# Waiting for x by tiles, and rounding turned outputs one pass earlier, in a two-block transformer kernel

## The reference

```
h = rmsnorm(x, g_mix_norm)
proj = h @ w_in                       # (256 x 1024) by (1024 x 6664)
...
o = g[0] * o_compressed + g[1] * o_selected + g[2] * o_window
x = x + o.reshape(256, 1024) @ a_w_out
```

## Time and profile before

| what | value |
|---|---|
| time, median of 3 runs | 1104.09 us (1103.22 to 1106.47) |
| profiled execution: time, span | 1103.02 us, 1101.2 us |
| TensorE busy | 1093.2 us, 99% |
| VectorE, ScalarE, POOL busy | 620.5, 584.7, 139.1 us |
| TensorE's granted clock | 1.00 |
| DMA | 185.40 MB, mean 168 GB/s |

### The profile page before, as it was taken

How to read it: one execution, slowest core, us unless ns; L and a number is a source line. 1 busy time by engine, 2 the same in 40 slices (tenths; PEclk the granted TensorE clock), 3 DMA queues, 4 the chain that set the end, 5 groups by cost and what they waited for, 6 DMA issues and landing times.

```text
span 1101.2 us, 14119 instructions
## 1 busy us (share of the span) xinstructions
PE 1093.2 (99%) x5851; PEld 928.0 (84%) x5851; DVE 620.5 (56%) x687; ACT 584.7 (53%) x916; POOL 139.1 (13%) x203
## 2 busy tenths in 40 slices
PE   8999999999999999999999999999999999999998
PEld 6877888888999988888889888888889888888887
DVE  5544544467555545456667665555457866555442
ACT  6788654434555434346567364444447846444431
POOL 1031311110231100122320010000004400000000
PEclk9999999999999999999999999999999999999999
DMA  8843534455644555545141254554544345555451
GB/s 317 322 153 115 191 115 154 143 175 179 242 176 169 191 194 189 196 127 186 61 153 48 95 200 175 181 183 171 191 153 138 112 153 199 186 189 191 172 181 68
DMA packets 29232, 185.40 MB, mean 168 GB/s; under 512 B 3552, under 2 KB 3936, under 8 KB 9184
## 3 DMA queue, kind: packets, MB, share of 16 engines
q1 hardware_dynamic: 27344, 178.31, 45.6%
q0 software_dynamic: 1680, 5.92, 1.5%
q10 hardware_dynamic: 144, 0.26, 0.1%
HBM read 183.43 MB, written 1.05 MB: 168 GB/s over the span
## 4 chain that ended last, share of the span: by engine, by line
PE 94%; ACT 2%; DVE 2%; DMA 1%; SPq 0%; issue 0%; DVEq 0%
PE ps L590 24%; PE ps L593 24%; PE ps L592 24%; PE ps L570 5%; PE ps L724 3%; PE ps L643 3%; PE ps L642 3%; PE ps L641 3%; PE ps L705 3%; ACT t L1233 1%; DMA t<-in_w 1%; PE ps L945 1%; ACT t L1236 1%; DVE t L1836 1%; DVE t L1988 0%; PE ps L786 0%
## 5 line engine op out<-in xcount | busy, mean ns | idle before, releaser
L1836 DVE TENSOR_TENSOR t<-t 128x2048 fp32r<-128x2048 f32 (+8 forms) x287 | 414.4, 1458 | 341.9 <-ACT t L1236 339.7
L1236 ACT ACTIVATE t<-t 128x2048 fp32r<-128x2048 f32 (+7 forms) x255 | 337.9, 1348 | 278.8 <-PE ps L593 236.5
L590 PE MATMUL ps<-t 128*128 128x512 f32 (+2 forms) x1178 | 465.3, 395 | 2.2 <-DVE t L1879 1.5
L593 PE MATMUL ps<-t 128*128 128x512 f32 (+2 forms) x1178 | 457.4, 388 | 0.0
L592 PE MATMUL ps<-t 128*128 128x512 f32 (+2 forms) x1178 | 457.1, 388 | 0.2 <-DVE t L1836 0.2
L590 PEld LDWEIGHTS ps<-t 128*128 128x128 f32 x1178 | 221.3, 188 | 45.8 <-DVE t L1879 1.9
L593 PEld LDWEIGHTS ps<-t 128*128 128x128 f32 x1178 | 221.1, 188 | 45.7
L592 PEld LDWEIGHTS ps<-t 128*128 128x128 f32 x1178 | 221.5, 188 | 43.1 <-DVE t L1836 0.9
L2518 POOL TENSOR_TENSOR t<-t 128x32 f32<-128x32 f32 (+8 forms) x108 | 92.2, 865 | 505.2 <-ACT t L1233 449.0
L1233 ACT ACTIVATE t<-ps,t 128x256 f32<-128x256 f32 (+4 forms) x216 | 95.8, 453 | 90.8 <-DVE t L1988 45.2
L1836 DVE TENSOR_TENSOR t<-ps,t 128x512 fp32r<-128x512 f32 (+6 forms) x124 | 76.0, 633 | 27.6 <-ACT t L1236 25.2
(11 more groups left out here) (109 smaller groups left out, 543.2 us busy)
## 6 DMA issues: line engine op xcount, KB each, us to landing
t<-in_w SPq DMA_DIRECT2D x155, 1024.0 KB, 4.9
t<-in_w SPq DMA_DIRECT2D x12, 512.0 KB, 4.7
t<-in_w SPq DMA_DIRECT2D x5, 768.0 KB, 4.1
t<-in_g POOLq DMA_DIRECT2D x4, 512.0 KB, 9.4
t<-in_w SPq DMA_DIRECT2D x2, 640.0 KB, 3.8
t<-in_w SPq DMA_DIRECT2D x4, 256.0 KB, 4.4
t<-in_x SPq DMA_DIRECT2D x1, 1024.0 KB, 5.4
t<-in_memt POOLq DMA_DIRECT2D x1, 1024.0 KB, 9.8
```

The source lines that it names most:

```text
L590: e.matmul(o, sh, wh, start=k0 + j == 0, stop=False)
L593: t = e.matmul(o, sl, wh, start=False, stop=last and j == n - 1)
L1236: return e.activation(o, src, ACT.Copy, scale=scale)
L1836: return e.tensor_tensor(o, a, b, op)
```

## The change

Four edits. TensorE waits in chunks 1 to 3 for the rest of the one tile of x that the next products read. Chunk 3 is cut tile by tile by ScalarE and VectorE. SyncE issues the load of `m.X` when the first half of chunk 2 has landed. ScalarE writes the rounded part of the sparse attention's turned outputs in passes 25 and 29, at the start of the pass, ahead of the copy and the exponents; VectorE's part stays in passes 26 and 30.

```diff
 tensor_program
     gemm_first(x)
     for c in range(1, 4):
-        gemm(c, x, ready)
+        gemm(c, x, lambda k, h: after("lo of", "x", k))
 scalar_program
     split_gained("x", m.xT, "gmix", 1, m.HT)
-    cut(3)
+    cut_by_piece(3)
...
-        elif i in (26, 30):
-            split(("no", 0, (i - 26) // 4), m.o_lo[0][:, :, half((i - 26) // 4)])
+        elif i in (25, 29):
+            split(("no", 0, (i - 25) // 4), m.o_lo[0][:, :, half((i - 25) // 4)])
 vector_program
-    for c in range(3, 6):
+    cut_by_piece(3)
+    for c in range(4, 6):
         cut(c)
 sync_program
         if c == 3:
-            w.wait_ge(*after("ld", 2, 3))
+            w.wait_ge(*after("ld", 2, 1))
             e.dma_start(m.X[:], x_d.rearrange("o (h p) d -> p (o h) d", p=128)).then_inc(*whole(("ld x",)))
```

## The result

The changed kernel takes 1100.95 us (median of 8 runs, 1099.87 to 1102.63) beside 1103.89 us for the kernel before (8 runs, 1103.22 to 1106.47). The ratio is 0.9975, 95% interval 0.9966 to 0.9984, which is 2.9 us less: 0.27%. Timed again beside later experiments it took 1100.48 against 1103.62, ratio 0.9973 (0.9964 to 0.9983). The profiled execution has a span of 1099.2 and a time of 1101.06 us (before 1101.2 and 1103.02).

The account below looks back on a forecast made before the run. The prediction took TensorE, 94% of the chain, to bound the kernel, so only its stops count. Terms of 1.72 + 0 + 0 + 0.4 + 0.4 = 2.5 us took 1104.09 to 1101.6 us, range 1100.0 to 1104.3.

Parts of the forecast that it names:

- Edit 1: TensorE's stop between chunks 1 and 2, waiting for x's turned tiles, vanishes: gain 1.72 us, bounds 0 and 1.8.
- the slow restart: First product after TensorE's stop before chunk 2 takes 0.33 us instead of 0.23; 0.10 us gained if the stop goes.
- Edit 2: Chunk 3 on ScalarE and VectorE: cutting by tiles buys 0.16 to 2 us of margin and no time.
- Edit 3: x's load: issued 2.4 us earlier, landed at about 21.2 instead of 22.3; buys margin before chunk 5, no time.
- The mixing danger: First stage: x's megabyte mixes with chunk 2's second half and tile 7; full mixing would stop TensorE 2.0 us.
- rivals B and C: x shares DMA engines, TensorE stops in chunk 2: B 1103.3 us, chance 0.12; C, full mixing, 1104.8, chance 0.06.
- Rival C: Full mixing stops TensorE 2.0 + 0.1 us in chunk 2, plus block 27's held scores: 1104.8 us, chance 0.06.
- Edit 4, first place: Sparse attention, product of chunk 88 and values behind it: earlier rounding gains 0.4 us, bounds 0 and 0.77.
- Edit 4, second place: Sparse attention, before chunk 89: wait and restart vanish through an earlier join; gain 0.4 us, bounds 0 and 0.46.
- Rival A: Sparse attention: held copy, exponents of pass 25 and slip of pass 29 eat the rounding gain; 1102.4 us, chance 0.2.
- Sum: All edits: 1.72 + 0 + 0 + 0.4 + 0.4 = 2.5 us, giving 1101.6 us from 1104.09; chance 0.62.

Follow-up runs that it names:

- e2: Kernel before with only ScalarE's rounding of the turned outputs moved to passes 25 and 29: 1103.19 us, ratio 0.9992.
- e1: Kernel before with only the products of chunks 1 to 3 waiting for x's tiles one by one: 1103.12 us, ratio 0.9992.
- e3: Changed kernel with x issued only when the second half of chunk 2 has landed: 1102.40 us, ratio 0.9987.
- e4: Changed kernel with no wait before x's load, issued right behind chunk 3: 1101.05 us, ratio 0.9971.
- a0: Changed kernel as it is, timed again: 1100.48 us, ratio 0.9973.
- a7: Changed kernel with ScalarE's rounding in passes 25 and 29 behind the copy, ahead of the exponents: 1099.80 us, ratio 0.9967.
- e10: a7 with chunk 1 issued right behind chunk 0: 1101.50 us, ratio 0.9979.
- e9: Changed kernel with chunk 1 issued right behind chunk 0, without waiting for chunk 0's second tile: 1101.13 us, one run.
- e8: Changed kernel with POOL's two loads of constants issued only when x has landed: 1101.94 us, one run.
- e6: Changed kernel with VectorE's rest of the turned outputs also moved to passes 25 and 29: 1103.59 us, one run.

## Why the prediction was right, point by point

The forecast was 1101.6 us, 2.5 us less; measured were 2.9 and 3.1 us less. The mechanism was right for edits 1 and 4 and wrong for edit 3; the sizes follow.

- **Edit 1.** Right, in place and in size: 1.72 forecast, 1.78 from chunk 1's first product to chunk 5's. Tile 7 was ready 0.59 us before its time, where 0.49 was worked out. What I had not seen is what the gain is counted from. Before, the end of the stage hangs on the landing of chunk 2's second half: chunk 2 starts 2.81 us after it (16.91 to 19.72; in e2 2.80, 17.76 to 20.56). Now it hangs on chunk 0 and chunk 1's first tile, and its lateness (0.5 to 1.4 us of wait in seven of ten such profiles) goes into the time in full. By 2.81 us behind the landing at 17.33, the old order would have started chunk 2 at 20.14 in the execution profiled after, against 18.64: an estimate of 1.5 us, and 1.6 with the slow restart, where the forecast had 1.62 and 1.72.
- **Edit 2.** Right as far as it was tested: e1, with chunk 3 whole, has no wait in chunk 3.
- **Edit 3.** This is the step that failed, twice. "I take x as landed at about 21.2" was wrong by its rule: the hole of 0.3 MB at 18 to 19 us was taken for time that x gains. It was filled, and half of x's sixteen parts had landed by 21.2 (the eighth at 21.13, the ninth at 21.23). But ScalarE waits for the last part, and that one landed 2.9 us behind the last part of chunk 3 as before: the lagging part had no hole to fill. And the term "buys margin, no time" was too small. The rest of chunk 5 is done 9.84 us after x has landed (22.30 to 32.14 before, 26.65 to 36.49 in e2). Before, its second product came at 34.58, a margin of 2.4 us, and in e2, which has neither edit 1 nor edit 3, x came 3.5 us later than usual and went through that margin: the stop of 1.0 us. With edit 1 the margin is smaller, 0.4 us in e3's profile (33.85 to 34.26) and 0.8 in the changed kernel's, so the same late x would stop TensorE longer; no profile shows this happen. The highest runs of kernels that issue x late are 3.0 (before, its 30 runs beside e1 to e4), 1.6 (e1), 2.4 (e2) and 2.8 us (e3) above the median, those of kernels that issue it early 1.7 (changed), 0.6 (e4), 1.4 (a0), 0.4 (a7) and 0.6 (e10). Without edit 3 the median is 1102.40 (e3), with it 1100.95, 1101.05 (e4) and 1100.48. That earlier issue protects from a late x is argued from this and from one profile. Why four parts of x landed 3.5 us later there was not found, and the intervals of e3 (0.9977 to 0.9997) and a0 (0.9964 to 0.9983) overlap. A rival was not tested: the three highest runs of e3 (1103.86 to 1105.20) and the eight highest beside e1 to e4 of the kernel before have a granted clock of 0.998 over the run, and so has the changed kernel's highest (1102.63). No trace of such a run was kept, so it is open whether the lower clock makes these runs long or follows from a stop of TensorE in them. The nine runs of e3 at 0.999 or more have a median of 1101.82.
- **The mixing danger (rivals B and C).** Did not come. e4 goes further than the change and shows nothing of it. The Trainium skill (DMA: Bandwidth & Descriptors, Queues, rings and completion order) says that on each DMA engine descriptors are consumed in ring order, and promises no order of completion for the loads of one queue. The first half agrees with e4's trace: x issued at 10.86 still landed behind chunk 3, issued before it, each of its parts 2.56 to 2.92 us behind the part of the same rank of chunk 3. Rival C's sum was loose: it named 0.55 us of held scores "paid in full" and added 0.3. The waits in e9 are a warning that order of issue is not all: chunk 1, issued after chunk 0's tiles, made them late.
- **Edit 4, first place.** 0.4 forecast, 5.03 - 4.68 = 0.35 measured. The product of chunk 88 was to stand 595.9 - 591.99 = 3.9 us behind the turn, and stands 594.75 - 590.86 = 3.89 behind it. The held values of block 23 came 0.3 us late (592.63, 1.77 us behind the turn, and 593.46 - 591.99 = 1.47 before), where 0.3 was forecast. The scores of block 27 were held 2.93 - 2.30 = 0.63, where 0.56 was forecast.
- **Edit 4, second place.** 0.4 forecast, 5.19 - 4.82 = 0.37 measured. Together 0.75 in the distance, and the same in e3, e4, e8, e9 and a0 (0.78 to 0.86). Rival A, that the holds eat the gain, is out. e6 and a7 show how near it was: with VectorE moved too the holds cost 2.2 us, with the copy out of the way 0.5 us more is gained.
- **Sum.** In the profiles 1.78 - 0.58 + 0.75 = 1.95 of the 2.0 us of span. The timed difference is 0.9 us more, so that the total came close to the forecast is in part luck: the profiled pair gave less, and edit 3, priced at nothing, may give the difference. Edits 1 and 4 alone gave 0.6 and 0.5 us, which leaves more to edits 2 and 3 than their terms of nothing, but with intervals of up to 1.9 us each the runs do not settle how the 2.9 us divide.

## What to carry to other kernels

When a stop of the bounding engine goes away, look for the event that its time is counted from next: here it changed from the landing of one transfer to that of an earlier one, and its scatter came with it. A step moved forward on an in-order engine pays with what stands behind it; put it behind the short work that others already wait for and ahead of the long work that waits anyway (the copy first, then the rounding, then the exponents: 0.5 us). A load is there when its last part is: a hole in the traffic helps only if the part that lags can use it. An edit that only buys margin may be worth time in the median when the thing it guards is a transfer (argued here, not shown): price the margin against the scatter of landings, not against one profile.

## What the runs showed of the hardware

- The landings of the first stage keep nearly fixed distances: chunk 3 (1 MB) is taken up 2.5 us after the second half of chunk 2 (19.39 - 16.91, 19.82 - 17.33, 21.08 - 18.59 in e3), and x 2.6 to 3.0 us after chunk 3 in every profile but e2's (6.4), whether it is issued 2.5 (before), 4.7 (changed) or 9.1 us (e4) before chunk 3 is taken up.
- A load of 1 MB lands in sixteen parts that are spread over 1.5 to 2.8 us (chunk 3: 17.60 to 19.37 before, 18.01 to 19.80 changed, 18.45 to 19.91 in e4, 18.29 to 21.06 in e3). With x issued early, each part of x comes 2.6 us (the last 2.9) after the part of the same rank of chunk 3, and the spread stays.
- The DMA engines moved 119 GB/s in the microsecond from 18 to 19 with x issued at 16.91, and 401 with x issued 1.8 us sooner, and the last part of x landed no sooner behind chunk 3: a hole in the traffic is not yet time for the transfer behind it.
